# A fused two-block model on one core: the head norm of the GLA layer on a 128x6 table, earlier cached query blocks in layer 3, and one activation table for Exp and Ln

## What is computed

```
def gla_layer_mixer(x, mem, w_in, w_gate2, b_gate, head_g, w_mem_kv, w_out):
    q, k, v, r, glr, qm = jnp.split(x @ w_in, A_IN_SPLITS, axis=-1)
    log_g = jax.nn.log_sigmoid(glr @ w_gate2 + b_gate) / GLA_TAU
    o = gla_chunked(q * GLA_DK ** -0.5, k, v, log_g)          # per head
    o = o * lax.rsqrt(jnp.mean(jnp.square(o), axis=-1, keepdims=True) + EPS) * head_g[None, :, None, :]
    o = from_heads(o) * jax.nn.silu(r)
    m = memory_attention(qm, mem, w_mem_kv)
    return jnp.concatenate([o, m], axis=-1) @ w_out

def stick_breaking(q, k, v):      # per block of 128 queries
    z = q @ k.T * scale
    log_not = jnp.where(mask, jax.nn.log_sigmoid(-z), 0.0)
    log_A = jax.nn.log_sigmoid(z) + lax.cumsum(log_not, axis=3, reverse=True) - log_not
    A = jnp.where(mask, jnp.exp(log_A), 0.0)
    return A @ v

def peer(x, w_q, subkeys, u_tab, v_tab):   # 8 heads x 16 experts per token
    s = (x @ w_q) against subkeys; the 16 best of each half, the 16 best sums -> idx, g
    act = gelu(einsum('nd,nhkd->nhk', x, u_tab[idx]), approximate=False)
    return einsum('nhk,nhkd->nd', g * act, v_tab[idx])
```

## Time and profile before

| | us |
|---|---|
| median of 3 runs | 2485.86 |
| lowest, highest | 2484.33, 2491.89 |
| span of the profiled execution | 2479.3 |
| PE, DVE, ACT, POOL busy in it | 2219.9, 1662.4, 914.7, 887.3 |

### The profile page before, as it was taken

One profiled execution on the slowest core, in us unless ns is written; L12 is line 12 of the kernel. 1 busy time (PEld: TensorE's weight loads), 2 busy tenths in 40 slices (PEclk: granted clock), 3 DMA queues, 4 the chain that ended last, 5 costly groups with the idle time before them and its releaser, 6 DMA issues.

```text
span 2479.3 us, 30019 instructions
## 1 busy us (share of the span) xinstructions
PE 2219.9 (90%) x9846; PEld 1274.3 (51%) x9846; DVE 1662.4 (67%) x3975; ACT 914.7 (37%) x2664; POOL 887.3 (36%) x796
## 2 busy tenths in 40 slices
PE   9989999989898889898989898889999999977776
PEld 7877745545454445554545554445555545523223
DVE  3874576666665677666777666667667767777764
ACT  2232133332443343344443334433344533433232
POOL 0012043444433334333444343244443434344442
PEclk9999999999999999999999999999999999999999
DMA  5421599999999999999999999999999999999996
GB/s 197 133 73 36 197 385 426 426 426 426 426 424 424 422 400 426 424 425 424 409 410 426 425 424 425 387 426 426 425 425 397 409 426 426 425 427 427 427 425 286
DMA packets 151656, 942.31 MB, mean 380 GB/s; under 512 B 16864, under 2 KB 19136, under 8 KB 53072
## 3 DMA queue, kind: packets, MB, share of 16 engines
q0 software_dynamic: 110592, 805.36, 77.4%
q1 hardware_dynamic: 40912, 135.06, 14.1%
HBM read 939.30 MB, written 1.05 MB: 379 GB/s over the span
## 4 chain that ended last, share of the span: by engine, by line
PE 45%; DMA 38%; DVE 8%; ACT 5%; issue 3%; POOL 0%; DVEq 0%; ACTq 0%; POOLq 0%
DMA arena<-in_uv,idx 37%; PE bank L1929 26%; PE bank L371 6%; DVE arena L1957 4%; PE bank L1561 3%; PE bank L1573 2%; ACT arena L1997 1%; PE bank L843 1%; PE bank L866 1%; DMA weights<-in_sb_v 1%; DVE arena L1216 1%; PE bank L602 1%; ACT arena L1985 1%; PE bank L830 1%; ACT arena L1991 0%
## 5 line engine op out<-in xcount | busy, mean ns | idle before, releaser
L1929 PE MATMUL bank<-arena 128*128 128x512 f32 x3072 | 1426.7, 609 | 222.0 <-ACT arena L1997 213.6
L2018 POOL DMA_INDIRECT arena<-in_uv,idx x768 | 859.5, 1119 | 1370.7 <-PE bank L1929 1241.3
L1929 PEld LDWEIGHTS bank<-arena 128*128 128x128 f32 x3072 | 567.1, 193 | 917.3 <-issue 588.1
L1957 DVE CUSTOM_DVE_ANT_0 arena<-arena,h 128x1024 f32<-128x1024 f32 x512 | 627.5, 1226 | 377.5 <-DMA arena<-in_uv,idx 370.9
L1985 ACT ACTIVATE arena<-arena 128x2 f32<-128x2 f32 x384 | 78.1, 203 | 1133.4 <-DVE arena L1957 1133.1
L1957 DVE CUSTOM_DVE_ANT_0 arena<-arena 128x1024 f32<-128x1024 f32 x256 | 313.7, 1226 | 196.7 <-DMA arena<-in_uv,idx 185.9
L371 PEld LDWEIGHTS bank<-xT,weights 128*128 128x128 f32 x1808 | 250.6, 191 | 52.2 <-issue 35.1
L371 PE MATMUL bank<-xT,weights 128*128 128x128 f32 (+2 forms) x1808 | 269.3, 304 | 0.0
L1997 ACT ACTIVATE arena<-const,arena 128x128 f32<-128x128 f32 x768 | 260.5, 386 | 0.0
L1991 ACT ACTIVATE arena<-arena 128x1 f32<-128x1 f32 x768 | 184.9, 288 | 12.6
L1548 ACT ACTIVATE arena<-bank 128x128 f32<-128x128 f32 (+4 forms) x174 | 52.1, 307 | 136.1 <-PE bank L371 54.0
(11 more groups left out here) (333 smaller groups left out, 1884.8 us busy)
## 6 DMA issues: line engine op xcount, KB each, us to landing
weights<-in_w_q SPq DMA_DIRECT2D x42, 512.0 KB, 17.0
weights<-in_w_in SPq DMA_DIRECT2D x38, 512.0 KB
weights<-in_a_fm SPq DMA_DIRECT2D x28, 512.0 KB
arena<-in_uv,idx POOLq DMA_INDIRECT x768
weights<-in_a_out SPq DMA_DIRECT2D x16, 512.0 KB
weights<-in_b_fm SPq DMA_DIRECT2D x16, 512.0 KB
weights<-in_b_out SPq DMA_DIRECT2D x16, 512.0 KB
arena<-in_w_q SPq DMA_DIRECT2D x14, 512.0 KB, 13.0
```

What stands on the lines that cost most here:

```text
L1929: ins = nc.tensor.matmul(acc[:, :], diag[:, e % DIAGS, :], ring[:, e % RING, at:at + 512], start=first, stop=last)
L1957: V.tensor_tensor_reduce(out=u, in0=u, in1=x, scale=1.0, scalar=0.0, op0=ALU.mult, op1=ALU.add, accum_out=dots[:, unit % 2, kx:kx + 1]).th ...
L2018: nc.gpsimd.indirect_dma_start(out=ring[:, s, :], out_offset=None, in_=io[f"uv{unit // PH // NT}"], in_offset=bass.IndirectOffsetOnAxis(ap ...
```

## The change

- Head norm: TensorE now multiplies the squares of each head, as weights, by one column of ones, so that the sums of the 6 heads come out as a 128x6 table with tokens on partitions. VectorE's scale and reciprocal and ScalarE's root run on 128x6. TensorE then spreads each column over all partitions by a matmul with the identity, into two banks, and VectorE multiplies from there. VectorE's two small operations stand in slot 32 in front of the six L2505, the root in slot 33, the spread in slot 34 of TensorE, the final product in slot 34 of VectorE.
- The nine cached query blocks of layer 3 follow the first nine of the blocks b_q0, b_k0, b_q1, ... of the first tile in SP's queue; before, they followed the eight b_v blocks and the first b_out block.
- Before Exp and Ln a table with both is loaded by name.

```
@@ gla_tensor
-            for x in range(2):
-                pe.wait_ge(*banks.take(("os", i, x)))
-                out = banks.bank(("os", i, x))
-                nc.tensor.matmul(out[:, 0:384], ones, rs[:, 3 * x:3 * x + 3, :].rearrange("p a b -> p (a b)"),
-                                 start=True, stop=True).then_inc(banks.full_sem(("os", i, x)), 1)
+            pe.wait_ge(*banks.take(("os", i)))
+            out = banks.bank(("os", i))
+            for hd in range(6):
+                ins = nc.tensor.matmul(out[:, hd:hd + 1], rs[:, hd, :], ones[:, 0:1], start=True, stop=True)
+            ins.then_inc(banks.full_sem(("os", i)), 1)
             yield o + 33
             tm_piece(pe, "a_out", i, 7, cat[:, 7, :], D, False, False)
+            yield o + 34
+            pe.wait_ge(sem("o_rstd"), i + 1)
+            for x in range(2):
+                pe.wait_ge(*banks.take(("or", i, x)))
+                out = banks.bank(("or", i, x))
+                for hd in range(3):
+                    at = HEAD_RSTD + 3 * x + hd
+                    ins = nc.tensor.matmul(out[:, hd * P:(hd + 1) * P], bc(small[:, at:at + 1], (0, P)), ident,
+                                           start=True, stop=True)
+                ins.then_inc(banks.full_sem(("or", i, x)), 1)
             for kc, at in enumerate((36, 36, 37, 38, 39, 40)):
                 yield o + at
-                pe.wait_ge(sem("o_gated"), i + 1)
+                for x in range(2):
+                    pe.wait_ge(*banks.emptied(("or", i, x)))
@@ gla_scalar
             act.wait_ge(sem("gate_abs"), i + 1)
+            nc.scalar.preload_act_table_set("natural_log_exp_and_others")
...
-            yield o + 34
+            yield o + 33
             act.wait_ge(sem("o_var"), i + 1)
-            nc.scalar.activation(rs[:, :, :], rs[:, :, :], ACT.Sqrt).then_inc(sem("o_rstd"), 1)
+            head_rstd = small[:, HEAD_RSTD:HEAD_RSTD + 6]
+            nc.scalar.activation(head_rstd, head_rstd, ACT.Sqrt).then_inc(sem("o_rstd"), 1)
@@ gla_vector
             yield o + 32
+            head_rstd = small[:, HEAD_RSTD:HEAD_RSTD + 6]
+            v.wait_ge(*banks.full(("os", i)))
+            V.tensor_scalar(head_rstd, banks.bank(("os", i))[:, 0:6], 1.0 / GLA_DV, 1e-5, ALU.mult,
+                            ALU.add).then_inc(banks.emptied_sem(("os", i)), 1)
+            v.wait_ge(*banks.emptied(("os", i)))
+            V.reciprocal(head_rstd, head_rstd).then_inc(sem("o_var"), 1)
...
             yield o + 34
-            v.wait_ge(sem("o_squares"), i + 1)
             for x in range(2):
-                v.wait_ge(*banks.full(("os", i, x)))
-                out = banks.bank(("os", i, x))
-                ins = V.tensor_scalar(rs[:, 3 * x:3 * x + 3, :], out[:, 0:384].rearrange("p (a b) -> p a b", a=3),
-                                      1.0 / GLA_DV, 1e-5, ALU.mult, ALU.add)
-                ins.then_inc(banks.emptied_sem(("os", i, x)), 1)
-            for x in range(2):
-                v.wait_ge(*banks.emptied(("os", i, x)))
-            V.reciprocal(rs[:, :, :], rs[:, :, :]).then_inc(sem("o_var"), 1)
-            yield o + 35
-            v.wait_ge(sem("o_rstd"), i + 1)
-            V.tensor_tensor(cat[:, 0:6, :], rf[:, :, :], rs[:, :, :], ALU.mult).then_inc(sem("o_gated"), 1)
+                v.wait_ge(*banks.full(("or", i, x)))
+                V.tensor_tensor(cat[:, 3 * x:3 * x + 3, :], rf[:, 3 * x:3 * x + 3, :],
+                                banks.bank(("or", i, x))[:, 0:384].rearrange("p (a b) -> p a b", a=3),
+                                ALU.mult).then_inc(banks.emptied_sem(("or", i, x)), 1)
@@ sb_scalar, softplus and att_exp
+                if q == 0:
+                    nc.scalar.preload_act_table_set("natural_log_exp_and_others")
...
                 if q == 2:
                     act.wait_ge(*banks.full(("o3", i, 0)))
+                else:
+                    nc.scalar.preload_act_table_set("natural_log_exp_and_others")
@@ the blocks that the cached ones follow
-                      2: [("b_v", 0, kc) for kc in range(KC)] + [("b_out", 0, kc) for kc in OUT_ORDER]}
+                      2: [(name, 0, j) for j in range(6) for name in ("b_q", "b_k")] + [("b_v", 0, kc) for kc in range(KC)]}
```

More of the change, by code:

```diff
@@ L59 @@
 GLA_DV = 128
+HEAD_RSTD = 48
 MEM_H = 4
```

## The result

The changed kernel takes 2504.99 us (median of 4 runs, 2502.79 to 2510.17), the kernel before 2486.87 (the three runs listed above and one more). The ratio is 1.0076 with a 95% interval of [1.006, 1.0093]: slower by 18 us. The forecast was 2495.5.

What follows compares the result with a forecast made beforehand. DMA engines at 426 GB/s were taken to bound the ring part. Head norm +16, cached blocks -5 and tables -1.3 gave +9.7 us on the 2479.3 span, 2489.0, plus 6.6 around it: 2495.5 us, range 2482 to 2506.

Steps and rivals of the forecast that it cites:

- Same-slot reads empty the chain twice: Layer 2's head norm: VectorE waits for TensorE in slots 32 and 34; slot 35 starts 7.1 and 8.8 us later.
- The clock: Layer 2's tiles: TensorE's clock drops after both stalls, one drop more than before, 1.5 to 2.9 us, taken as 2.
- The head norm's size: Layer 2's two tiles: +7 and +9 us, together +16, after 2 us off each tile for weights landing meanwhile.
- the reserve: Layer 2's stalls: about 4 us of queued gathers cover the first part; both versions spend it once.
- Rival B: Layer 2's head norm: queued gathers cover the first stall, clock drops once; +3 to +5 a tile, total 2487; chance 0.24.
- The cached blocks: Layer 3's first tile: moving nine query blocks forward removes the wait for b_v, -5 us; bounds -5.3 and +4.
- rival D: Layer 3's b_q and b_k starve in addition, with the head norm's full price: +24 us, 2512; chance 0.04.
- the four stretches: Layers 2 and 3, both tiles: throughput below 426 GB/s loses 3.8, 4.5, 5.3 and 6.6 us, together 20 to give back.
- The tables: ScalarE: eight loads go, only one on the path, around 1904 in layer 3's second tile: -1.3 us; bounds 0 and -2.6.
- its two bounds, -5.3 and -2.6: Lower bounds for layer 3's moved query blocks and for the Exp and Ln table; the range's lower end took 9 off.

Runs made afterwards that it cites:

- experiment with late reads: Kernel before with the new head norm alone, VectorE reading sums in slot 34, spread made in 35 and read in 37: 2486.63 us, ratio 1.0001.
- the kernels with one read kept: New head norm alone with only its first or only its second same-slot read, against the kernel before: 2489.48 us, 1.0013, and 2486.79 us, 1.0005.
- whole change with late reads: All three parts, VectorE reading sums in slot 34 and the spread in 37, against the kernel before: 2486.55 us, ratio 1.0003.
- the experiment's profile: Kernel before with one table for Exp and Ln as the only change: 2483.71 us, ratio 0.9995.
- the changed kernel's second one: The changed kernel as it is, measured once more against the kernel before: 2498.89 against 2485.05 us, ratio 1.0055.

## Why the prediction was right, and where it was not

**Same-slot reads empty the chain twice: right, step by step.** Forecast were 7.2 us of idle VectorE (863.1 - 855.9), TensorE stalls of 6.7 and 4.9 us in the first tile, and two gaps of GpSimd. The trace has 7.26, 6.52 and 4.89. GpSimd's gaps are 10.48 and 8.80 us. The experiment with late reads shows that these waits make the loss. From the sums to slot 35 the forecast was 7.1 and 8.8 us later, with 2 more for the clock; it is 8.4 and 11.0 in all, of which eight records at 5.38 and 6.10 instead of 3.60 us are 1.8 and 2.5.

**The clock: right.** After both stalls the next matmuls run slower, the first time 5.38 us for eight, the second 8.83 for sixteen, where 7.20 is full speed; the kernel before shows this once a tile. The Trainium skill (TensorE: Matmul & The Clock Gate, "HAM oscillation — how this bites in real kernels") had that pattern, and the case that the first trace did not show, two in a row, has now been seen to agree.

**The head norm's size: +16 forecast, +13.4 measured alone**, 18 by the marks in the changed kernel's profile (+8.4, and +12.0 less the 2.3 that the moved blocks add there). This term was in range, but the picture behind its size was wrong: both versions were taken to spend the reserve once, with 2 us a tile off for weights. The reserve is worth more than that. The kernel before already had one stall of 6.23 and 4.39 us per tile, and the late version without it is no faster within the 0.15% of its interval, so that first stall was nearly free. What the change adds is a second one inside the time of refilling, which begins with 2.0 gathers in flight instead of 2.8.

**Rival B (the queued gathers cover the first stall):** its mechanism is real and its conclusion is not. It priced the pair at +3.5 us a tile; the kernels with one read kept cost 2.1 and 0.8 a tile, the pair 6.7. It took for the pair about what the two cost singly.

**The cached blocks: the step that failed.** "So the 5.3 us of 1580 to 1610 go: I take -5." They do go, the changed kernel has no wait for in_sb_v in that tile, and nothing starves at b_q (rival D does not occur), but the medians differ by 0.1 us, and the wrong way, with an interval from -2.5 to +4. The premise behind it, that a byte which is late is never made up and that the four stretches are therefore 20 us to be had, is what was wrong. The cached blocks take away the 5.3 us at their place, the late reads take 3.0 of 4.0 and 2.1 of 4.8 us in the 55 us around the stalls, and no kernel became measurably faster. The shortfall reappears: at the layer norm for the cached blocks (above), and for the late norm in part in smaller pieces. In the whole change with late reads, 30 us stretches counted from the mark lack 1.0, 0.4 and 1.3 us around the former dip of 3.6 in the first tile, and that tile takes 377.1 us against 376.9. For the cached blocks the count of gathers shows how: a queue that was never empty at b_v has landed 5 us more of them by 1651, TensorE is at the same slot, and so the next stalls are met with 2.4 in flight instead of 4.4. For the late norm this was not counted out, and stays argued.

**The tables: -1.3 forecast.** The ratios say -1.2 alone (0.9995) and -0.7 on top of the cached blocks (1.0003 to 1.0000); both are inside the noise, so the size is not settled. The stall at the place named is 1.3 us shorter. Between the marks the six profiles with the new tables have 361.9 to 363.0 us in layer 3's second tile, the eight without scatter from 362.3 to 368.3; the means are 362.5 and 365.4, which speaks for a gain there, though not for its size. In the experiment's profile ScalarE's next operation starts 1.29 us after the load's start (1904.13 to 1905.42). The price of a switch in the Trainium skill (ScalarE: Activation LUTs, "What ACT_TABLE_LOAD costs"), by which this term would have been -2.7, is not borne out by that.

**Sum.** Forecast +16 - 5 - 1.3 = +9.7, measured +18.1 and +13.8. The head norm was up to 3 us off in either direction, and the 5 us counted too much are the cached blocks. The first measurement, 2504.99, lies 1 us inside the upper end of the range, which it owes to the allowance for rival D, a case that did not occur. At the lower end the working takes 9 us off where its two bounds, -5.3 and -2.6, make 7.9.

## What to carry to other kernels

- When a value made by another engine is read in an in-order schedule, look at what stands behind the reader. Reading in the slot in which it is made saved nothing here and stopped everyone behind it; two slots later the same work cost nothing that could be measured.
- In a kernel bound by a ring of prefetches, ask of every stall how long ago the last one was. One of 4.3 or 6.5 us a tile cost 0.05 or 0.13% here (the smaller is not told from nothing), two within 17 us 0.55%, two within 27 us 0.34%.
- A stretch with less than full throughput is an upper bound of what may be gained, not a gain. Before counting it, look behind it for a stretch in which the engines set the pace: here the late bytes were made up there. Compare stretches at the same place of the program, not at the same time.

## What was not expected of the hardware

Code at the same place can differ between single executions by several microseconds, because transfers land later. At the start of layer 2's first tile, in code that is long before its head norm, six of the nine profiles with the new norm lack 1.9 to 3.6 us of throughput in the first 60 us, as in this row of the head norm alone, and none of the five without it do (425 GB/s before):

```profile
690.00:710.00 20.00, 17.28 (x65) 9.10 (x64) 13.05 (x34) 5.31 (x19) 6.17 (x6) 0.91 1.02 361
```

The DMA engines are busy there throughout (share 1.02) and move less, and VectorE waits for gathers 7.2 us in these 20 us, where it waits 4.8 at the same place before. Three profiles of the new norm, the changed kernel's second one among them, show 0.7 us or less, so the same code can run there without it. Its cause stays open. It is one reason to take sizes from medians and only mechanisms from the trace.
